# Second attention of a two-block kernel: head 0's queries loaded during the recurrence, one queue for bias, keys and masks, maxima turned by one matmul

## What is computed

```python
def dsa_attention(q, c, qi, ki, wi, rel_bias, w_uk, w_uv):      # 8 heads, 16 meta keys + 2048
    s_idx = ...                                                 # index scores, causal
    _, sel = lax.top_k(s_idx, 256)                              # per query, shared by all heads
    lg_s = (q_lat . c[sel]) * scale + rel_bias[t5_bucket(q_pos - sel)]
    lg_m = (q_lat . c_meta) * scale + rel_bias[...]
    p = softmax(concat([lg_m, lg_s]))
    return p . c  -> w_uv
def second_block(...):
    a = dsa_attention(...) * silu(gate_a)
    r = rms_norm(hgrn2(q_h, f_h, i_h, lb)) * silu(gate_h)
    h = layer_norm(alpha * h + concat([a, r]) @ w_out)
```

## Time and profile before

| | |
|---|---|
| three executions | 3507.53, 3513.32, 3513.90 us, median 3513.32 |
| the profiled execution | 3512.26 us, its span 3510.1 us |
| busy in the span | PE 91%, DVE 63%, ACT 40%, POOL 26% |
| recurrence ends, second attention starts | about 2697 us |
| second attention | to about 3303 us of the span |

### The profile page before, as it was taken

How to read it: one execution, slowest core, us unless ns; L and a number is a source line. 1 busy time by engine, 2 the same in 40 slices (tenths; PEclk the granted TensorE clock), 3 DMA queues, 4 the chain that set the end, 5 groups by cost and what they waited for, 6 DMA issues and landing times. The chain is left out here.

```text
span 3510.1 us, 43583 instructions
## 1 busy us (share of the span) xinstructions
PE 3209.4 (91%) x15232; PEld 2461.1 (70%) x15232; DVE 2200.2 (63%) x4305; ACT 1410.1 (40%) x2383; POOL 896.8 (26%) x828
## 2 busy tenths in 40 slices
PE   4999999799999998988789999997896899999798
PEld 4799888666666666876568878886774566666577
DVE  7111111267777776332489999986673789998766
ACT  5000001144444444221258998242554233333454
POOL 0111111257555460000421323334232111211000
PEclk9999999899999998999899999998998899999999
DMA  5322223476565433445311344454134523422344
GB/s 210 105 80 68 87 83 120 125 158 142 123 143 115 114 73 123 150 136 197 79 40 56 102 152 137 118 164 173 50 112 126 158 58 76 92 62 55 125 149 134
DMA packets 331916, 400.80 MB, mean 114 GB/s; under 512 B 100324, under 2 KB 249188, under 8 KB 319124
## 3 DMA queue, kind: packets, MB, share of 16 engines
q1 hardware_dynamic: 260376, 299.09, 30.0%
q10 hardware_dynamic: 67488, 78.03, 7.4%
q0 software_dynamic: 3840, 20.98, 2.6%
HBM read 265.39 MB, written 132.62 MB: 113 GB/s over the span
## 5 line engine op out<-in xcount | busy, mean ns | idle before, releaser
L2232 PE MATMUL f_pO<-f_PT,f_vv 128*128 128x512 f32 (+3 forms) x944 | 375.5, 480 | 0.0
L2262 ACT ACTIVATE f_PT<-f_pS 128x512 f32<-128x512 f32 (+3 forms) x472 | 222.9, 472 | 334.2 <-PE f_pS L2200 152.7
L2892 DVE TENSOR_SCALAR_CACHE_REDUCE sharedI<-xI,TI 128x768 bf16<-128x768 f32 (+10 forms) x276 | 339.6, 1296 | 5.4 <-DVE TI L2898 5.2
L2696 PE MATMUL cbank<-hT_high,cw_hi 128*128 128x512 f32 x800 | 319.0, 399 | 18.9 <-DVE cw_lo L2851 6.8
L2262 ACT ACTIVATE n_PT<-n_pS 128x512 f32<-128x512 f32 (+4 forms) x352 | 177.4, 504 | 360.3 <-PE n_pS L2212 196.6
L585 PE MATMUL p_bank<-hT_high,p_w_hi 128*128 128x512 f32 (+1 forms) x768 | 304.6, 397 | 16.1 <-DVE p_w_lo L708 16.1
L2696 PE MATMUL cbank<-hT_high,cw_lo 128*128 128x512 f32 x800 | 315.8, 395 | 0.0
L2696 PE MATMUL cbank<-hT_low,cw_hi 128*128 128x512 f32 x800 | 315.4, 394 | 0.0
L2232 PE MATMUL n_pO<-n_PT,n_vv 128*128 128x512 f32 (+4 forms) x704 | 307.3, 518 | 0.0
L585 PE MATMUL p_bank<-hT_low,p_w_hi 128*128 128x512 f32 (+1 forms) x768 | 303.4, 395 | 0.0
L585 PE MATMUL p_bank<-hT_high,p_w_lo 128*128 128x512 f32 (+1 forms) x768 | 302.5, 394 | 0.0
(11 more groups left out here) (421 smaller groups left out, 7410.6 us busy)
## 6 DMA issues: line engine op xcount, KB each, us to landing
f_zz<-scratch_z ACTq DMA_DIRECT2D x128, 128.0 KB, 3.2
c_w_first<-in_w_in_dram SPq DMA_DIRECT2D x26, 512.0 KB, 4.6
cw_raw<-in_w_in_dram SPq DMA_DIRECT2D x25, 512.0 KB, 4.3
p_w_raw<-in_w_in_dram SPq DMA_DIRECT2D x22, 512.0 KB, 4.1
lent<-scratch_qkb POOLq DMA_DIRECT2D x40, 256.0 KB, 10.2
scratch_z<-p_stage ACTq DMA_DIRECT2D x32, 256.0 KB, 2.4
scratch_qk_high<-p_stage ACTq DMA_DIRECT2D x32, 256.0 KB, 2.6
scratch_qk_low<-p_stage_low ACTq DMA_DIRECT2D x32, 256.0 KB, 3.2
```

The lines of the kernel that those rows point to most:

```text
L2232: pe.matmul(pO[:, B % 2, c0:c1], lhsT=vv[0:nk, b, kt, :], rhs=PT[0:nk, u % PR, c0:c1], start=(kt == 0 and not heads[h].local), stop=(heads ...
L2262: act.activation(PT[0:nk, u % PR, c0:c1], pS[0:nk, u % SR, c0:c1], ACT.Exp, scale=0.125).then_inc(s_ex, 1)
L2696: last = pe.matmul(bank[:, p % RING, 0:wd], lhsT=w_part[pw][b][:, c, :], rhs=rhs, start=(c == 0 and a == 0), stop=(c == DC - 1 and a == 2))
L2892: own_.up(v.tensor_scalar(junk_v[:, own_.at % 2, 0:(i + 1) * P], scores(i), T[:, j:j + 1], None, compare, ALU.add, accum_out=count[:, j:j ...
```

## The change

The recurrence lends part of its room from `lent`, which is now allocated before it. On SP, at the step ("turn", 3), it loads head 0's queries of the second attention into that room. In the second attention ACT copies both high parts of head 0's queries, DVE subtracts for the low part, POOL blanks QA[0] and no longer cuts head 0's queries. SP alone loads, in one row, bias, keys, masks and turned masks of block 0, low keys, masks of block 1, values, turned masks of block 1, and so on. Only two gates are loaded at the start, in both attentions, the other two after the first exponential. The four maximum columns of a block lie in columns 0, 32, 64 and 96 of one 128x128 tile, one matmul turns them, and ACT copies four rows of 128 (second attention only).

```diff
@@ stage_recur(..., lift, room, next_queries)
-        rbB, tab = m.sb("rbBL", [BUCKETS, 2, P]), m.sb("tabL", [BUCKETS, 2, PITCH])
-        bv = m.sb("bvL", [P, 2, PITCH])
+        tab = room[0:BUCKETS, E:E + 2 * PITCH].rearrange("p (z u) -> p z u", z=2)
+        rbB = room[0:BUCKETS, E + 2 * PITCH:E + 2 * PITCH + 2 * P].rearrange("p (z k) -> p z k", z=2)
+        bv = room[:, E + 1024:E + 1024 + 2 * PITCH].rearrange("p (z u) -> p z u", z=2)
...
-        F, KS, PW, VT = two("FG", [P, E]), two("KSG", [P, E]), two("PWG", [P, total]), m.sb("VTG", [P, E])
+        F, KS, PW, VT = two("FG", [P, E]), two("KSG", [P, E]), two("PWG", [P, total]), room[:, 0:E]
...
@@ SP, in the loop over seq
+                if (step, h) == ("turn", GH - 1):
+                    sp.wait_ge(s_mv, GH)
+                    for half in (slice(0, HD), slice(HD, P)):
+                        sp.dma_start(room[half, 0:S], next_queries).then_inc(s_next, 16)
...
+            sp.wait_ge(s_next, 32)
@@ stage_attend
-        Mx = m.sb(n_("Mx"), [P, 4, P], F32R)
+        Mx = m.sb(n_("Mx"), [P, 4 if rel is None else 1, P], F32R)
+        Mx_columns = Mx[:, :, 96] if rel is None else Mx[:, 0].rearrange("p (r c) -> p r c", r=4)[:, :, 0]
@@ SP, load_head(h)
-                if rel is not None:
-                    if h >= 1:
-                        sp.wait_ge(s_part, 2 * h)
+                if rel is not None and h >= 1:
+                    if h == 1:
+                        sp.wait_ge(s_fh, 2 * NJ)
+                        sp.wait_ge(s_fl, NJ)
+                    else:
+                        sp.wait_ge(s_part, 2 * (h - 1))
                     for half in (lower, upper):
                         sp.dma_start(rq[half], hd.q[0]).then_inc(s_rq, 16)
...
                 if h == 0 and rel is not None:
                     load_masks(0)
+                    load_turned_masks(0)
@@ SP, start (load_turned_masks is now SP's, its body otherwise the same)
             load_head(0)
+            if rel is not None:
+                load_masks(1)
             load_values(0)
             if rel is not None:
-                for j in range(1, NJ):
+                load_turned_masks(1)
+                for j in range(2, NJ):
                     load_masks(j)
+                    load_turned_masks(j)
                 load_bias(1)
@@ POOL
+            if rel is not None:
+                step(gp.memset(QA[0][HD:P, :].bitcast(F32), 0.0))
+                gp.sem_inc(s_blank[0], 1)
...
                 split_bias(h)
-                split_queries(h)
+                if h >= 1:
+                    split_queries(h)
@@ PE, max_scores, turn_max, scores
+                if rel is not None and h == 0 and n == sw.chunk0[j]:
+                    pe.wait_ge(s_fh, j + 1)
...
-                for r in range(4):
+                for r in range(4 if rel is None else 1):
                     last = pe.matmul(pR[:, r], lhsT=Mx[:, r], rhs=ident_r[:], start=True, stop=True)
...
+                    if rel is not None and h == 0:
+                        pe.wait_ge(s_fh, NJ + j + 1)
+                        pe.wait_ge(s_fl, j + 1)
@@ ACT
-                act.activation(QA[h % NB][96:P, j * QB4:(j + 1) * QB4], pR[96:P].rearrange("p a b -> p (a b)"), ACT.Copy
-                               ).then_inc(s_mr, 1)
+                if rel is None:
+                    last = act.activation(QA[h % NB][96:P, j * QB4:(j + 1) * QB4], pR[96:P].rearrange("p a b -> p (a b)"),
+                                          ACT.Copy)
+                else:
+                    for r in range(4):
+                        at = j * QB4 + r * P
+                        last = act.activation(QA[h % NB][96:97, at:at + P], pR[32 * r:32 * r + 1, 0], ACT.Copy)
+                last.then_inc(s_mr, 1)
...
-            for B in range(GATES):
+            if rel is not None:
+                for j in range(NJ):
+                    at = slice(j * QB4, (j + 1) * QB4)
+                    act.activation(QA[0][lower, at], rq[lower, at], ACT.Copy).then_inc(s_fh, 1)
+                for j in range(NJ):
+                    at = slice(j * QB4, (j + 1) * QB4)
+                    act.activation(QL[0][upper, at], rq[upper, at], ACT.Copy).then_inc(s_fh, 1)
+            for B in range(2):
                 load_gate(B)
             act.wait_ge(s_const, 1)
-            if rel is not None:
-                load_turned_masks(0)
             for u in steps():
                 if 0 <= u < U:
                     exps(u)
-                    if rel is not None and u == 0:
-                        for j in range(1, NJ):
-                            load_turned_masks(j)
+                    if u == 0:
+                        for B in range(2, GATES):
+                            load_gate(B)
@@ DVE
-            own_.up(v.memset(QA[0][HD:P, :].bitcast(F32), 0.0))
+                for j in range(NJ):
+                    at = slice(j * QB4, (j + 1) * QB4)
+                    v.wait_ge(s_fh, j + 1)
+                    v.tensor_tensor(QL[0][lower, at], rq[lower, at], QA[0][lower, at].bitcast(F32), ALU.subtract
+                                    ).then_inc(s_fl, 1)
```

More of the change, by code:

```diff
@@ L1954, in load_masks, with load_turned_masks @@
                     sp.dma_start(chosen[:, at], MK[:, at]).then_inc(s_mk[j], 16)
+            def load_turned_masks(j):
+                tiles = list(sw.tiles(0, j))
+                first, last = MASK_AT[j, 0], MASK_AT[j, tiles[-1]]
+                nk, end = sw.keys(j, tiles[-1]), last + QB4 - mask_tile_col(j, tiles[-1])
+                sp.dma_start(mkt[:, first:last], MKT[:, first:last]).then_inc(s_mt[j], 16)
+                sp.dma_start(mkt[0:nk, last:end], MKT[0:nk, last:end]).then_inc(s_mt[j], 16)
             if local_no:
@@ L1982, in _ @@
                 if j == 0 and h == NH - 1:
-                    sp.wait_ge(s_part, 2 * (NH if rel is not None else len(local_no)))
+                    sp.wait_ge(s_part, 2 * (NH - 1 if rel is not None else len(local_no)))
                     for to, src, loaded in ahead:
@@ L2149, in max_scores @@
                     else:
-                        pe.wait_ge(s_part, 2 * h + 1)
+                        if h >= 1:
+                            pe.wait_ge(s_part, 2 * h - 1)
                         pe.wait_ge(s_hi[b], 16 * plain_no[h] + 16)
@@ L2248, in _ @@
         def _(act):
-            def load_turned_masks(j):
-                tiles = list(sw.tiles(0, j))
-                first, last = MASK_AT[j, 0], MASK_AT[j, tiles[-1]]
-                nk, end = sw.keys(j, tiles[-1]), last + QB4 - mask_tile_col(j, tiles[-1])
-                act.dma_start(mkt[:, first:last], MKT[:, first:last]).then_inc(s_mt[j], 16)
-                act.dma_start(mkt[0:nk, last:end], MKT[0:nk, last:end]).then_inc(s_mt[j], 16)
             def exps(u):
@@ L2363, in max_columns @@
                     a, b = min(r for r, p in runs if p == n), max(r for r, p in runs if p == n) + 1
-                    last = v.tensor_reduce(Mx[:, a:b, 96], mxc[:, B % 2, a:b, 0:n], AX.X, ALU.max)
+                    last = v.tensor_reduce(Mx_columns[:, a:b], mxc[:, B % 2, a:b, 0:n], AX.X, ALU.max)
                 last.then_inc(s_stat, 1)
@@ L2394, in _ @@
             v.memset(KA[0][96:97, :].bitcast(F32), -1.0).then_inc(s_blank[0], 1)
-            own_.up(v.memset(QA[0][HD:P, :].bitcast(F32), 0.0))
-            own_.settle()
-            if heads[0].cum is not None:
-                own_.up(v.memset(QA[0][HD:HD + 2, :].bitcast(F32), 1.0))
+            if rel is None:
+                own_.up(v.memset(QA[0][HD:P, :].bitcast(F32), 0.0))
                 own_.settle()
-            v.sem_inc(s_blank[0], 1)
+                if heads[0].cum is not None:
+                    own_.up(v.memset(QA[0][HD:HD + 2, :].bitcast(F32), 1.0))
+                    own_.settle()
+                v.sem_inc(s_blank[0], 1)
+            else:
+                for j in range(NJ):
[3 more added lines that the diff above has]
+                                    ).then_inc(s_fl, 1)
             if local_no:
@@ L3064, in build_program @@
         m = Memory(nc, last, used)
-        lent, s_lent = m.sb("lent2", [P, DC // 2, D]), [m.sem(f"o2_w_lent{i}") for i in range(DC // 2)]
+        lent = m.sb("lent2", [P, DC // 2, D])
+        stage_recur(nc, used, QH, FH, FHm, IV, IVm, lb_raw, hgrn_norm_g, RRT,
+                    (CK, CKm, kv_norm_g, w_uk, w_uv, rel_bias, (buckets, buckets_turned), KTs, VE, (BV, BVT)),
+                    lent[:].rearrange("p a b -> p (a b)"), latent(0).q[0])
+        clear(nc, used)
+        s_lent = [m.sem(f"o2_w_lent{i}") for i in range(DC // 2)]
         chosen = m.sb("n_chosen", [P, OFF[NT] + NT * NMETA], BF16)
```

17 lines of the change are left out of this document (9 added, 8 removed).

## The result

| | kernel before | changed kernel |
|---|---|---|
| first comparison, median of 5 runs each | 3512.66 us | 3488.21 us |
| ratio, 95% interval | | 0.9941, 0.993 to 0.9952 |
| repeated later | median 3510.14 (11 runs) | 3483.45 (5 runs), ratio 0.9926, 0.9913 to 0.9939 |
| all runs of the two kernels | median 3510.1 (60 runs) | median 3486.1 (10 runs) |
| profiled execution | 3512.26 us | 3490.18 us, span 3488.5 us |

The change makes the kernel 24 us, 0.6 to 0.7%, faster. The page of the changed kernel, part 1, against the earlier trace rows: PE has 96 matmuls less, ACT 104 instructions more.

The account below looks back on a forecast made before the run. The second attention's start was taken as bound by loads, the rest by PE with DVE close behind. Gains of 9.5 + 6 + 4 + 0.6 = 20.1 us gave 3493.2 us by the median, range 3481 to 3505.

Parts of the forecast that it names:

- Part 1: Second attention up to the first score: fewer bytes ahead of block 1's masks, 9.5 us earlier, bounds 5 and 12.
- Part 2: Second attention, first score to step 9: turned-mask wait goes, less new losses, 6 us gained, bounds -1 and 8.
- The wait and the clock: After the first score: DVE's turned-mask wait gone, 6.5 us, plus 1.5 us of PE's half clock behind it.
- POOL beside DVE: After the first score: POOL cutting head 1's queries beside a working DVE costs 1 us (0 to 5).
- "hair" at block 3's masks: Block 3's masks arrive 19 us after block 1's, needed 19.9 us after: no wait, but by a hair.
- Part 3: Turn of the maxima, second attention: one matmul for four saves 4 us (0 to 11).
- Part 4: First attention: two gates moved, PE starts 2 us earlier, but POOL limits the gain to 0.6 us (0 to 2).
- Recurrence at nothing: Loading the queries' 1.05 MB in the recurrence, where nothing waits for loads, costs nothing; at most 4.8 us.
- loads don't set the end: Rival: loads still set the end of the start, gain only 6.5 us, 3507; chance 0.11.
- ACT isn't held: Rival: ACT held 14 us issuing late gates in each attention, 8 us lost, 3521; chance 0.06.
- PE isn't the bound everywhere: Rival: PE bounds everywhere, the turn gives 11 us and part 1 12 us, 3483; chance 0.10.
- The rule of the Trainium skill: DMA engines alternate between queue rows with work; late gates would lengthen the wait at block 2's masks by 2.4 us.

Follow-up runs that it names:

- The order alone: Kernel before with only SP's loader order changed (block 1's masks ahead of values, turned masks moved from ACT's queue to SP's): median 3502.08 us, ratio 0.9976.
- the late gates alone: Kernel before with only the gate loads of blocks 2 and 3 moved behind the first exponential, in both attentions: median 3505.38 us, ratio 0.9987.
- the turn alone: Kernel before with only the turn of the maxima changed to one matmul and four ACT copies: median 3503.93 us, ratio 0.9987.
- without the order: Changed kernel with the old loader order back (values ahead of block 1's masks, turned masks on ACT's queue): median 3490.96 us, against 3483.45 beside it.

## Why the prediction was right

It said 3493, range 3481 to 3505; it came to 3488.21, and by all ten runs to 3486.1. The gain was 24 us where 20.1 was summed. By its parts, with means of the two profiles of either kernel:

- **Part 1, first score 9.5 us earlier.** Measured 10.0 (45.7 to 35.7 after the recurrence's end). The parts alone give 4.4 (queries, summed as 4.8), 1.6 (gates, 2.4), 3.3 (values out of the way, 2.4) and 1.1 for the turn, which was not in this sum; 10.4 together. Each is one profile against two of before that are 1.4 apart, so the parts are known to about 1 us. The masks of block 0 came much earlier than the 2710 that was named, at 2703.39. Of those 13.7 us, 3.7 are the earlier end of the recurrence (2683.41 against 2687.11), and the rest is 10.0 where 7.2 was summed. The order alone brings them 2.4 to 3.5 us forward, which the sum had left out. That gave nothing, since block 1's masks set the first score: it comes 7.3 to 7.4 us behind them in all 14 profiles.
- **Part 2, 6 us.** Measured 6.0 from the 1st to the 71st matmul (48.6 to 42.6), but that is luck in part: two terms in it were too small and cancel. At the prediction's own mark, step 9 (the 31st matmul, 2761.05 before), the gain is 8.6 us (27.51 and 27.43 before, 18.81 and 18.85 changed), over the 6 and over its upper bound of 8. The wait and the clock: 8 us was summed for both, of them 1.5 for the clock, while 9.0 came up to the 46th (33.2 to 24.2), and with the 1 us of loss at block 2's masks 7 was forecast there. PE's idle time is 5.7 us of it and its busy time 3.4; six matmuls of two turns are gone, an estimated 0.7 to 1.4 us (0.12 us each at full clock, about 0.23 at half, from 0.93 us for the four at 2736.88 before), so 2.0 to 2.7 are the clock's. POOL beside DVE: 1 us was taken, 3.0 measured (18.4 against 15.4 to the 71st), inside the 0 to 5 given; it came behind step 9. The "hair" at block 3's masks held. The clock did not stay at full level without a fall, as the prediction had it: it fell once more at 2758 in the first profile, not in the second.
- **Part 3, the turn, 4 us.** Measured 3.8. Read from the first pair of profiles alone it had looked like 1.4. ACT's four copies, estimated at 0.7 us, take 1.10.
- **Part 4, 0.6 us, capped by POOL.** The cap is shown by the late gates alone. The profiles with late gates reach the first local head at 792.6 to 794.2, those without at 793.8 to 795.3, and end the first attention's scores 1.3 us earlier on the mean, though the one with late gates alone doesn't (1361.8 against 1361.8 and 1360.1): 0 to 2 us, not settled.
- **Recurrence at nothing.** The 3.4 us by which it was shorter in the first pair are the clock's fall, which comes and goes. The choice stage took 4.2 us longer in the first pair (710.7 against 706.5 from its first matmul to its last); it takes 705 to 711 us over kernels that don't touch it, so that is scatter in size.

The profiles give 18.3 us from the recurrence's end to the last score, and 1.5 before it (means of 2683.8 and 2682.3). That is the distance of the executions that were profiled (means of 3508.0 and 3488.1, 19.9 apart). The medians of all runs give 24.0. So the other 4 us aren't placed: they lie between the executions profiled and the rest. The means of the recurrence (283.2 us in five profiles of its old place, 282.5 in nine of the new) would give 0.7, within scatter.

The rivals: loads don't set the end (one new wait, 1.43 us); ACT isn't held, and its four issues leave DVE waiting 0.78 us; PE isn't the bound everywhere (3.8 us of the 11). The rule of the Trainium skill, "DMA: Bandwidth & Descriptors", section "Queues, rings and completion order", would have put 2.4 us more at block 2's masks. The wait there is 1.43 us, near the 1 us of the sum. That is no test of the rule: the late gates were issued at 2721.20, when those masks had arrived (2720.22), a thing that the times of the prediction would have shown.

## What to carry to other kernels

Where one queue feeds a start that is bound by loads, write down for each tile when it is needed and when it arrives by bytes over the measured rate, and order by need; here that was worth more than the bytes taken away. Cost a wait with what the clock does around it: removing a wait of 4.8 to 6.5 us gave 9 to 10, since PE had also run at half clock behind it. Count the issues that an engine makes between two operations that others wait for, here ten of ACT's, behind which DVE waited 3.5 us. Ask what used to hide in the wait: POOL's cutting was free there and cost 3 us afterwards. And take a second profile of the kernel before: differences of 3 us in stages that the change doesn't touch came and went.

## What the runs showed of the hardware

- TensorE's granted clock can fall to 0.50 in a stretch of the recurrence in some executions of one kernel and not in others, and such recurrences were 3 to 8 us longer: 42 matmuls in 12 us where another execution has 79.
- The length of PE's stop doesn't tell whether the clock falls: the turn alone fell 6 us after the first score behind stops of PE of 0.39 and 0.98 us, the kernel before had one of 1.20 us there and stayed at 1.00 until its stop of 6.51 us.
- Beside POOL's subtractions of 64x512 DVE's multiply of 128x512 took up to 1.73 us instead of 0.68 (1.47 on the mean of 20 beside such operations, 0.91 beside POOL's other work); with POOL's plain copies alone the stretch was 1.5 us longer than with none, in one profile.
- ACT's copy of one row of 128 takes 0.27 us, four of them 1.10, against 0.59 for 32x512.
- SP was held 9.22 us in the issue behind the values (14.01 us and most of 22.17 before). No issue of ACT falls into these holds. Four do in another, in the first attention of the changed kernel: SP stood in one issue from 706.74 to 739.83 at a DMA share of 1.03, and the four gate issues of ACT's queue in that time took 0.47 to 0.62 us each.
- Issues that nothing holds still take ACT's time: ten between two exponentials 5.1 us (without the order), six 2.7 (before), four 2.4 (changed).
